# Three of layer 0's pairs of projection tiles by seven products, raw first key tiles, and a norm in two halves

## The reference

```python
for l in range(2):                                   # first block, two layers
    mx = split((silu(c) @ w_mod[l] + b_mod[l]), 6)   # modulation of x: shift, scale, gate, twice
    mc = split((silu(c_ctx) @ w_mod[l] + b_mod[l]), 6)
    zx = modulate(rms_norm(x, norm1_g[l]), mx[0], mx[1]) @ w_in[l]
    zc = modulate(rms_norm(ctx, norm1_g[l]), mc[0], mc[1]) @ w_in[l]
    # columns of z: Fourier 256, query latent 256, key/value latent 128, rope key 32, conv a 256, conv gate 256
    ...                                              # attention, Fourier mixing, gated convolution of 31 taps, w_o
    ctx = ctx + mc[5] * mlp(modulate(rms_norm(ctx, norm2_g[l]), mc[3], mc[4]))   # not in the last layer
    x = x + mx[5] * mlp(modulate(rms_norm(x, norm2_g[l]), mx[3], mx[4]))         # relu squared, 1024 -> 4096 -> 1024
# second block: three mixers, then cross attention to a memory of 256 tokens, then a gated feed-forward
mem_n = rms_norm(mem, norm_mem)
kv = mem_n @ xa_wkv                                  # keys and values, 1024 -> 2048
```

## Time and profile before

| | us |
|---|---|
| median of 3 runs | 1803.23 (1799.43 to 1803.93) |
| the profiled execution | 1798.18 |
| its span, first to last instruction | 1796.4 |
| TensorE busy | 1720.8 (96%) |
| VectorE busy | 980.5 (55%) |
| ScalarE busy | 415.9 (23%) |
| mean granted TensorE clock, of full | 0.992 |

### The profile page before, as it was taken

The page is one execution under the profiler, slowest core; times in us unless marked ns, Lnnn a source line. Parts: engine busy times, 40 slices in busy tenths (PEclk is TensorE's granted clock), DMA queues, the critical chain, the costliest instruction groups (busy, mean ns, idle before and its releaser), DMA issues.

```text
span 1796.4 us, 27176 instructions
## 1 busy us (share of the span) xinstructions
PE 1720.8 (96%) x10930; PEld 1379.4 (77%) x10930; DVE 980.5 (55%) x1881; ACT 415.9 (23%) x806; POOL 315.4 (18%) x349
## 2 busy tenths in 40 slices
PE   7999999899999999899899999999999999999997
PEld 5434454488888888665799998877888788799996
DVE  1238652365676434577378754377731432288883
ACT  1312553222111210226322101322421101211110
POOL 0100262122001221005134201068000000001110
PEclk9999999999999999999999999999999999999999
DMA  7784472232333222330345545434222443344452
GB/s 281 298 322 192 142 272 105 71 117 94 116 119 117 88 77 94 140 135 30 117 163 167 165 166 187 141 118 141 95 72 72 146 160 118 109 152 162 164 181 101
DMA packets 38710, 256.32 MB, mean 143 GB/s; under 512 B 4128, under 2 KB 7328, under 8 KB 9024
## 3 DMA queue, kind: packets, MB, share of 16 engines
q1 hardware_dynamic: 36240, 240.87, 38.3%
q0 software_dynamic: 1776, 9.57, 1.4%
q10 hardware_dynamic: 576, 4.19, 0.6%
HBM read 247.28 MB, written 7.34 MB: 142 GB/s over the span
## 4 chain that ended last, share of the span: by engine, by line
PE 84%; DVE 8%; ACT 2%; DMA 2%; issue 1%; POOL 1%; SPq 0%; ACTq 0%; DVEq 0%; POOLq 0%
PE ps L668 83%; DMA ring<-weights 1%; PE ps L901 1%; POOL aux L1912 1%; DMA xT<-x_t 1%; DVE arena L2121 1%; DVE aux L2150 1%; DVE arena L2151 1%; DVE arena L2152 1%; ACT hT L1527 0%; POOL aux L1895 0%; DVE ring L2195 0%; DVE aux L2055 0%; DVE aux L2057 0%; DVE aux L2060 0%
## 5 line engine op out<-in xcount | busy, mean ns | idle before, releaser
L668 PE MATMUL ps<-hT,ring 128*128 128x256 f32 (+3 forms) x3024 | 670.7, 383 | 16.8 <-ACT hT L1527 4.7
L668 PEld LDWEIGHTS ps<-hT,ring 128*128 128x128 f32 (+1 forms) x3024 | 520.2, 191 | 155.0 <-issue 97.3
L668 PE MATMUL ps<-arena,ring 128*128 128x256 f32 (+3 forms) x1884 | 355.4, 343 | 4.7 <-DVE arena L2152 3.4
L668 PEld LDWEIGHTS ps<-arena,ring 128*128 128x128 f32 (+1 forms) x1884 | 298.5, 191 | 50.9 <-issue 13.0
L668 PE MATMUL ps<-arena,sums 128*128 128x128 f32 (+1 forms) x966 | 161.6, 317 | 1.3 <-DVE aux L2221 1.3
L668 PEld LDWEIGHTS ps<-arena,sums 128*128 128x128 f32 x966 | 141.7, 191 | 12.3 <-DVE aux L2221 2.5
L1895 POOL TENSOR_TENSOR aux<-aux 128x256 f32<-128x256 f32 (+1 forms) x46 | 49.3, 1072 | 439.9 <-ACT aux L1462 370.9
L2194 DVE TENSOR_TENSOR sums<-ring 128x512 f32<-128x512 f32 x83 | 57.6, 694 | 66.5 <-PE ps L668 59.3
L668 PE MATMUL ps<-hT,sums 128*128 128x128 f32 (+1 forms) x592 | 89.9, 300 | 0.5 <-DVE aux L2221 0.5
L1912 POOL TENSOR_SCALAR aux<-aux,small 128x512 f32<-128x512 f32 (+1 forms) x48 | 71.0, 1486 | 86.9 <-DVE small L2170 86.3
L1931 POOL TENSOR_TENSOR arena<-arena 128x256 f32<-128x256 f32 (+1 forms) x32 | 26.4, 826 | 333.8 <-ACT arena L1651 333.8
(11 more groups left out here) (368 smaller groups left out, 1934.6 us busy)
## 6 DMA issues: line engine op xcount, KB each, us to landing
ring<-weights SPq DMA_DIRECT2D x224, 1024.0 KB, 4.9
kept_turns<-aux ACTq DMA_DIRECT2D x4, 1024.0 KB, 5.7
arena<-kept_turns POOLq DMA_DIRECT2D x6, 512.0 KB, 6.3
kept_keys_values<-spare POOLq DMA_DIRECT2D x1, 2048.0 KB, 8.2
arena<-kept_keys_values POOLq DMA_DIRECT2D x1, 2048.0 KB, 9.2
tab<-tables SPq DMA_DIRECT2D x1, 1344.0 KB, 13.9
arena<-mem_t SPq DMA_DIRECT2D x2, 512.0 KB, 5.5
xT<-ctx_t SPq DMA_DIRECT2D x1, 1024.0 KB, 9.1
```

The source lines that it names most:

```text
L668: ins = nc.tensor.matmul(o_, lhsT, rhs, start=start, stop=stop, skip_group_check=True)
```

## The change

1. **Projection of layer 0 by pairs.** Tiles 6, 7, 2 and 3 stay plain; the pairs (8,9), (0,1) and (4,5) use seven products, each from one whole chunk (`whole()` pads the stream). Modulation blocks come in halves of one chunk, in bursts of 2, 3, 3, 2, 3, 0 and 3 behind the items. VectorE forms four operands from `hT`, and the weight sums and recombinations of three pairs. 24 taps come before the latents, with sums and a recombination between them, 16 after the rope, 22 in the attention.
2. **Raw first key tiles.** Keys 0 and 1 are made from the memory times the gain without 1/root (`memg`); TensorE's order is key 0, `mst`, key 1, block 0, block 1, keys 2 to 5. VectorE multiplies both tiles by 1/root when it empties them. In the stream keys 0 and 1 are chunk 0. On SyncE's queue each half of the memory goes ahead of chunks 0 and 1.
3. **Second norm of layer 0 by sequence.** Reciprocal and scaling of the context's 256 columns, then those of x.

```diff
+KEYS_RAW = 2
-TAPS_EARLY = (46, 34)
-TAPS_MIDDLE = (0, 16)
+TAPS_EARLY = (24, 34)
+TAPS_MIDDLE = (16, 16)
+TAPS_PARTS = (6, 20)
+Z_FIRST = ((6, 2), (7, 3), ((8, 9), 3), (2, 2), ((0, 1), 3), (3, 0), ((4, 5), 3))
+Z_SEVEN = (4, 0, 2)
...
+    keys(0, KEYS_RAW)
     mod(0, 0)
-    keys(0, 2)
     mod(0, 1)
-    keys(2, 6)
+    keys(KEYS_RAW, 6)
...
+        if l == 0:
+            part = 2 * MOD_FIRST
+            for item, halves in Z_FIRST:
+                if isinstance(item, tuple):
+                    whole()
+                    p = item[0] // 2
+                    for role in range(4):
+                        for j in range(4):
+                            k, n = j + 4 * (role % 2), item[role // 2]
+                            out.append((("zq", 0, 0, p, 0, role, j), "w_in", 0, z_tile(0, n, k)))
+                else:
+                    for k in range(KD if item != 3 else KD // 4):
+                        out.append((("z", 0, item, k), "w_in", 0, z_tile(0, item, k)))
+                for _ in range(halves):
+                    mod(0, part // 2, 4 * (part % 2), 4 * (part % 2) + 4)
+                    part += 1
...
-            open_bank(("mst", 0), "hold")
-            for k in range(KD):
-                pe.wait_ge(S["mem_squares"], k + 1)
-                mm(bank(("mst", 0))[:, 0:T], ones, memsq[:, k, :], k == 0, k == KD - 1, ("mst", 0) if k == KD - 1 else None)
...
+            for n in range(KEYS_RAW):
+                key = ("xk", n)
+                o_ = open_bank(key)
+                for k in range(KD):
+                    pe.wait_ge(S["mem_gained"], k + 1)
+                    mm(o_[:, 0:T], weight(("xk", 0, n, k)), memg[:, k, :], k == 0, k == KD - 1, key if k == KD - 1 else None)
+                if n == 0:
+                    open_bank(("mst", 0), "hold")
+                    for k in range(KD):
+                        pe.wait_ge(S["mem_squares"], k + 1)
+                        mm(bank(("mst", 0))[:, 0:T], ones, memsq[:, k, :], k == 0, k == KD - 1, ("mst", 0) if k == KD - 1 else None)
             pe.wait_ge(S["silu_c"], 2)
             mod_block(0, 0)
-            mem_keys(0, 2)
             mod_block(0, 1)
-            mem_keys(2, 6)
+            mem_keys(KEYS_RAW, 6)
...
+                def z_quad(p):
+
+                    n_quad = quad_first[0, 0, "zq", p, 0]
+                    for i, (wf, af) in enumerate(PRODUCTS):
+                        b, o = divmod(i * T, 512)
+                        key = ("zq", 0, 0, p, b)
+                        if o == 0:
+                            open_bank(key)
+                        for j in range(4):
+                            r = z_act(af, j, n_quad == 0)
+                            if wf in ROLES:
+                                lhsT = weight(("zq", 0, 0, p, 0, ROLES[wf], j))
+                            else:
+                                lhsT = sums[:, n_quad % 2, SUMS[wf], j * P:(j + 1) * P]
+                            if i == 2 and j == 0:
+                                pe.wait_ge(S["quad_sums"], n_quad + 1)
+                            mm(bank(key)[:, o:o + T], lhsT, r, o == 0 and j == 0, j == 3,
+                               key if j == 3 and (o + T == 512 or i == 6) else None)
...
+                    for i, (item, halves) in enumerate(Z_FIRST):
+                        if isinstance(item, tuple):
+                            z_quad(item[0] // 2)
+                        else:
+                            z_plain(item, i == 0)
+                        if item == 3:
+                            latent_sums()
+                        for _ in range(halves):
+                            mod_block(0, part // 2, 4 * (part % 2), 4 * (part % 2) + 4)
+                            part += 1
+                    kr_sum(0)
+                    mod_turn(0, 1)
...
+                if l == 0:
+                    dve.wait_ge(S["h_ready"], KD)
+                    b11, b12 = hT[:, 0:4, half_a(0)], hT[:, 0:4, half_b(0)]
+                    b21, b22 = hT[:, 4:8, half_a(0)], hT[:, 4:8, half_b(0)]
+                    did(tt(z_form[0], b12, b11, ALU.subtract), "z_forms")
+                    did(tt(z_form[1], b22, b12, ALU.subtract), "z_forms")
+                    did(tt(z_form[2], b22, z_form[0], ALU.subtract), "z_forms")
+                    did(tt(z_form[3], b21, z_form[2], ALU.subtract), "z_forms")
+                    weight_sums(0)
                 finished(dve, ("z", l, 6))
                 did(v.memset(upad[:, :, :, :], 0.0))
+                if l == 0:
+                    combined(0, "zq", 0, Z_SEVEN[0])
...
-                for tap, k in rest[:TAPS_EARLY[l]]:
+                for n, (tap, k) in enumerate(rest[:TAPS_EARLY[l]]):
+                    if l == 0 and n == TAPS_PARTS[0]:
+                        weight_sums(1)
+                    if l == 0 and n == TAPS_PARTS[1]:
+                        combined(0, "zq", 0, Z_SEVEN[1])
                     conv_tap(tap, k)
+                if l == 0:
+                    weight_sums(2)
...
-                scaled(2 * l + 1, s, ("st", 2 * l + 1))
+                if l == 0:
+                    taken(dve, ("st", 1))
+                    for sd, name, order in ((0, "scaled", (0, 1, 2, 3, 4, 5, 6, 7)), (1, "scaled_x", (4, 5, 6, 7, 0, 1, 2, 3))):
+                        ss = slice(sd * T, (sd + 1) * T)
+                        did(v.reciprocal(rinv[:, ss], rinv[:, ss]))
+                        for k in order:
+                            did(v.tensor_tensor(hT[:, k, ss], xT[:, k, ss], rinv[:, ss], ALU.mult), name, wait=False)
...
-            for i in range(2):
-                sp.dma_start(memn[:, 4 * i:4 * i + 4, :], mem_in[:, 4 * i:4 * i + 4, :]).then_inc(S[f"mem_loaded{i}"], 16)
             for c in range(SLOTS):
+                if c < 2:
+                    sp.dma_start(memn[:, 4 * c:4 * c + 4, :], mem_in[:, 4 * c:4 * c + 4, :]).then_inc(S[f"mem_loaded{c}"], 16)
                 sp.dma_start(ring[:, c, :, :], weights[c, :, :, :]).then_inc(landed[c], 16)
```

More of the change, by code:

```diff
@@ L699, in mod_block @@
                 key = ("modp", l, part)
-                if q == first:
+                if q == first and k0 == 0:
                     open_bank(key, "mod")
@@ L792, in _, with z_act, z_plain @@
                     mod_block(1, MOD_LATE + 2, 0, 4)
-                for i, n in enumerate(Z_ORDER):
-                    if l == 1 and i == 2:
-                        mod_block(1, MOD_LATE + 2, 4, KD)
-                    if l == 1 and i == 4:
-                        mod_turn(1, 1)
+                def z_act(form, j, first):
+                    if form in ("b11", "b21", "b22"):
+                        return hT[:, j + (0 if form == "b11" else 4), half_b(0) if form == "b22" else half_a(0)]
+                    f = ("t1", "t3", "t2", "t4").index(form)
+                    if first and j == 0:
+                        pe.wait_ge(S["z_forms"], f + 1)
+                    return z_form[f][:, j, :]
+                def z_quad(p):
[15 more added lines that the diff above has]
+                               key if j == 3 and (o + T == 512 or i == 6) else None)
+                def z_plain(n, first):
                     key = ("z", l, n)
@@ L801, in _, with ready @@
                     o_ = open_bank(key)
-                    def ready(k, i=i, n=n, l=l):
-                        if i == 0:
+                    def ready(k):
+                        if first:
                             pe.wait_ge(S["h_ready"], KD * l + k + 1)
@@ L1002, in _ @@
                     w = width(l)
-                    if n_quad == 1:
+                    if l == 0 and n_quad == quad_first[0, 0, "m1", 0, 0] + 1:
                         give_back()
@@ L1523, in modulated_halves @@
                 order = [(k, 0) for k in range(KD)] + [(k, 1) for k in (4, 5, 6, 7, 0, 1, 2, 3)] if l == 0 else [(k, 1) for k in range(KD)]
-                for k, sd in order:
-                    act.wait_ge(S["scaled"], KD * norm + k + 1)
+                for i, (k, sd) in enumerate(order):
+                    if l == 0 and sd == 1:
+                        act.wait_ge(S["scaled_x"], i - KD + 1)
+                    else:
+                        act.wait_ge(S["scaled"], KD * norm + k + 1)
                     o_ = hT[:, k, sd * T:(sd + 1) * T]
@@ L1549, in _, with z_out @@
                             "h_ctx_ready", wait=False)
-                for i, n in enumerate(Z_ORDER):
+                def z_out(n, l=l, s=s):
                     key = ("z", l, n)
@@ L1898, in _ @@
             square_sum(0, slice(0, 2 * T))
+            for n in range(KEYS_RAW):
+                taken(pool, ("xk", n))
             for half in range(2):
@@ L2081, in _, with weight_sums @@
             quad_done = [0]
+            def weight_sums(n):
+                c, b = quad_chunk[n], n % 2
+                dve.wait_ge(landed[c % SLOTS], 16 * (c // SLOTS + 1))
+                if n >= 2:
+                    dve.wait_ge(chunks_used, quad_chunk[n - 2] + 1)
```

(29 more changed lines are left out.)

178 lines of the change are left out of this document (105 added, 73 removed).

## The result

The changed kernel takes **1808.23 us** (median of 7 runs, 1806.23 to 1812.29) against 1803.23 before (median of 7, 1799.43 to 1803.93). The ratio is 1.0040, 95% interval 1.0029 to 1.0052: slower, by 5.0 us between the medians and 7 by the ratio. The forecast was 1810 in a range of 1803 to 1820, with "slower" at 0.67. Span against span of the two profiled executions the change costs 9.7 us (1806.1 against 1796.4).

A forecast was written before the change was run, and what follows sets the result against it. TensorE, busy 96% of the span, was taken as the bound. Projection +1.8, attention +0.3, start +3.8, norm -1.4 gave +4.5, with the clock's +4.8 +9.3, put on the mean 1801.2: 1810 us, range 1803 to 1820.

The forecast's parts named there:

- A chunk is usable 6.0 us after the third chunk before it is started: Weight stream, ring of four slots: a chunk is usable about 6.0 us after TensorE starts the third chunk before it.
- Three waits of 3.25: Layer 0's projection: bursts of three half blocks make waits ahead of pair (8,9), tile 2 and tile 3, +9.75 us.
- Seven products and the old order's stalls: -7.9: Layer 0's projection: three pairs save 5.1 us, fewer changes between z and modulation 0.3, old stalls 2.5, together -7.9.
- VectorE: nothing: Projection and first score: 23 us more VectorE work, yet no TensorE wait; 2 us to spare after the rope.
- The start: +3.8: Raw first keys: keys 2 start at 30.4 us instead of 26.60, +3.8, between 2.8 and 4.8.
- Nothing later gives it back: After the start: its +3.8 us stays lost, as x itself is loaded behind the delayed chunks.
- The norm: -1.4: Second norm of layer 0 by sequence: the form TensorE waits for ends at 359.4, not 360.77, -1.4 us.
- The clock: two falls of four, 2.4 us each: Four places with waits of 3 to 5 us: the granted clock falls at two, +4.8 us, bounds 0 and 12.

The follow-up runs named there:

- e10: The changed kernel run once more with nothing edited, with a second trace: 1810.39 us, ratio 1.0046 to the kernel before.
- e3: The kernel before with only the new order of tiles and bursts in layer 0's projection, all tiles plain, no seven products: 1813.72 us, ratio 1.0066.
- e1: The changed kernel with the projection's half blocks spread 1, 2, 2, 2, 2, 2, 2 and 3, the 1 ahead of tile 6: 1803.14 us, ratio 1.0009.
- e8: e7 with latents' sums behind tile 3's half blocks, one half block moved from behind tile 7 to ahead of tile 6, (0,1) recombined after 10 taps, not 14: 1803.73 us.
- e9: e8 with the start of the kernel before in place of the raw key tiles, the norm by sequence kept: 1800.65 us, ratio 0.9991 to the kernel before.
- e11: e8 run once more with nothing edited, for a trace of its slower group of executions: 1806.5 us, ratio 1.0028 to the kernel before.
- e2: The changed kernel with its start put back as in the kernel before, the other two parts as changed: 1805.95 us, ratio 1.0025.
- e4: The kernel before with only the second norm of layer 0 done by sequence: 1799.93 us, ratio 0.9993.
- e5: The changed kernel with keys 2 to 5 behind the first modulation block and keys 6 and 7 behind the second: 1810.73 us, ratio 1.0055.
- e6: e5 with x loaded behind chunk 7 instead of chunk 11: 1806.93 us, ratio 1.0036 to the kernel before.
- e7: The spread projection of e1 put behind the start of e6: 1801.48 us, ratio 1.0007 to the kernel before.

## Why the prediction was right

Right in sign and, for the projection, in mechanism. In size it is right by the spans (+9.3 forecast, +9.7 measured), which is what it was added up for; by the ratio the change costs 7 us (5 to 9), and 8 in e10 (6 to 11), so the forecast lies at the upper end of the one interval and inside the other. That the sum comes so near is in part luck: some of its terms were off in opposite directions, as the steps show.

- *A chunk is usable 6.0 us after the third chunk before it is started.* Burst to product is 6.05 us at tile 2 (127.24 to 133.29) and 6.20 at tile 3, and up to 6.48 in e10. Held.
- *Three waits of 3.25.* 0.75 + 2.56, 3.27 and 3.41: 9.99 us for 9.75. Held; e3 shows that the order alone makes them, and e1 that another order takes most of them away.
- *Seven products and the old order's stalls: -7.9.* The stage is 5.0 us longer; less 9.99 of waits and 2.8 for the slow pair (15.07 us from 112.17 to 127.24, where the other two take 12.28 and 12.18) that is -7.8. Held.
- *VectorE: nothing.* It never holds TensorE in the projection, and the idle time ahead of the first score is 2.19. Held, but only because of the bursts: in e1, which takes them away, the recombination of (0,1) is late and costs 2.40 us. Most of the slack was TensorE's lateness.
- *The start: +3.8.* This term was mis-sized, and the whole of the start came near it by luck: key tile 2 came 4.98 late. TensorE started at 9.78 where I had 9.4, the first key tile took 6.3 us and not 5.5, and from the first half block to keys 2 there passed 8.46 us (23.12 to 31.58) for the forecast 8.5. So the chain of chunks was right and the chain ahead of it was 1.2 short; the first tile lasts 5.1 to 6.3 us in the eight traces with this start, with a median near 5.6, so most of that is the chance of one execution; TensorE's start was late in all eight (9.78 to 10.43). "Nothing later gives it back" was wrong: the wait for x's sums shrank by 1.4 us. Together that is +3.6.
- *The norm: -1.4.* The form's product came 2.1 us sooner. What it is worth depends on where the clock falls, and it falls once there in every trace of the new norm. In e1, e8, e9, e10 and e11 it falls at the first products, as in the kernel before, and what that costs is hidden in the wait for the form: 19.9 us from the last half block to the second pair, 22.0 before, so -2.1. In the change, e2, e4, e5, e6 and e7 it falls behind that wait, where nothing hides it: 21.3 to 21.5, so -0.7 to -0.5. The forecast lies between, and had not asked where the fall would stand.
- *The clock: two falls of four, 2.4 us each.* Two of four, 2.8 and 2.1, 4.9 for 4.8. As a share it holds further: in the six traces with the bursts of three (the change, e2, e3, e5, e6, e10) the clock falls behind 10 of the 18 waits ahead of a z tile or pair, for some 1.5 to 3 us each: five times at pair (8,9), three at tile 2, two at tile 3. e10 shows the same kernel with other falls. The Trainium skill (page "TensorE: Matmul & The Clock Gate", section "HAM oscillation — how this bites in real kernels") describes a kernel in which each such un-hidden DMA wait costs a fall. e3 agrees with that at all three places, the changed kernel does not at tiles 2 and 3, and in all 8 of the 18 waits passed without a fall. No run here tells what decides it.

Still open: what sets the place of a fall, and with it some us of any comparison of two single traces (8.4 between two of the same program). The price of part 2 is open too: taking it back starts the first z tile 5.2 us sooner in e2's trace, but gives only 2 to 4 us in the medians, and part 2 alone was not run in the kernel before.

## What to carry to other kernels

Count a stream of weights in slots and not in bytes: when a slot is freed by the use of the next chunk, what costs is a run of chunks used up faster than one can land, three in 2.8 us against 6.0 here, and the loss can be read beforehand off any other place in the trace with that pattern. Removing such a wait uncovers what was late just behind it (here VectorE's recombination, then x's load), so follow the next engine before adding the gains up. And compare stages by their waits and work at one clock first, then add the clock as a spread, not as a term.

## What the hardware showed that I had not expected

The granted clock of one and the same program falls in different places from one execution to the next, behind the same idle times: at 111 us in one trace of the changed kernel and not in the other, at tiles 2 and 3 the other way round; in e8 nowhere before 353 us, in e11 three times, which puts it 5.7 us behind by then. It can fall behind 1.45 and 0.91 us of waits among small products (288.5 in the changed kernel, not in e10, whose waits there are the same), and hold behind 3.4 us (160.66).

The first key tile, 16 records of 256 columns, took 6.50 us at 9.78 with the granted clock read as 1.00 there, against 3.62 for the next 16. The first products of the kernel before are slow too, on other data. Over all thirteen traces the first 16 records take 5.26 to 6.50 us, whichever product comes first.
